# Attention values of two heads as two column tiles of 64 instead of one matmul of 128 columns

## The reference

```python
# first block: 8 sparse heads (values shared by all heads) and 8 forgetting heads
return jnp.einsum('bhqk,bqkd->bqhd', probs, v_sel)      # dsa
return jnp.einsum('bhqs,bshd->bqhd', probs, vb)         # fox
# second block, two layers: 4 heads on a memory of 256 tokens in each, 12 block-sparse heads in layer 1
o = jnp.einsum('bhsm,bmhd->bshd', p, v)                 # mem
return (jnp.einsum('bhcjk,bhcjkd->bhcd', p_sel, v_sel)
        + jnp.einsum('bhck,bhkd->bhcd', p_own, v_own))  # moba
```

## Time and profile before

| | |
|---|---|
| median of 3 runs | 830.77 us (830.05 to 831.02) |
| the profiled execution | 831.16 us |
| its span, first to last instruction | 829.3 us |
| granted clock of PE | 0.997 of full speed |
| PE busy | 817.7 us |
| DVE busy | 522.4 us |
| ACT busy | 427.8 us |

### The profile page before, as it was taken

How to read it: one execution, slowest core, us unless ns; L and a number is a source line. 1 busy time by engine, 2 the same in 40 slices (tenths; PEclk the granted TensorE clock), 3 DMA queues, 4 the chain that set the end, 5 groups by cost and what they waited for, 6 DMA issues and landing times.

```text
span 829.3 us, 11757 instructions
## 1 busy us (share of the span) xinstructions
PE 817.7 (99%) x4514; PEld 700.9 (85%) x4514; DVE 522.4 (63%) x654; ACT 427.8 (52%) x622; POOL 111.3 (13%) x144
## 2 busy tenths in 40 slices
PE   8999999999999999999999999999999999999997
PEld 7998987778878777899999998887667999999996
DVE  5646988767685757556555446687975655555451
ACT  5546656553655554364444444546685654444440
POOL 1600300000021510030000000069900000000000
PEclk9999999999999999999999999999999999999999
DMA  8951444355636633546555555464114466656541
GB/s 298 324 188 40 153 153 152 102 165 203 234 125 234 219 125 102 203 139 217 197 169 191 201 174 183 151 203 136 68 51 153 153 205 214 200 191 196 171 139 52
DMA packets 76503, 140.44 MB, mean 169 GB/s; under 512 B 2952, under 2 KB 22608, under 8 KB 76464
## 3 DMA queue, kind: packets, MB, share of 16 engines
q1 hardware_dynamic: 74352, 134.03, 48.4%
q0 software_dynamic: 1968, 5.82, 2.2%
q10 hardware_dynamic: 144, 0.07, 0.0%
HBM read 138.86 MB, written 1.05 MB: 169 GB/s over the span
## 4 chain that ended last, share of the span: by engine, by line
PE 89%; DVE 6%; ACT 2%; DMA 1%; issue 1%; POOL 0%; SPq 0%; ACTq 0%; DVEq 0%
PE bank L1729 55%; PE bank L2075 22%; PE bank L1877 3%; PE bank L1795 2%; DVE w_lo L1167 2%; PE bank L1931 1%; PE bank L1764 1%; PE bank L1847 1%; DVE tok L1335 1%; PE bank L1907 1%; DMA raw<-in_w_in 1%; PE bank L1932 1%; PE bank L1743 1%; DMA raw<-in_w_mem_kv 1%; DVE mx L1317 1%
## 5 line engine op out<-in xcount | busy, mean ns | idle before, releaser
L1167 DVE TENSOR_TENSOR w_lo<-raw,w_hi 128x2048 fp32r<-128x2048 f32 (+2 forms) x65 | 146.6, 2256 | 50.6 <-ACT w_hi L718 50.1
L1607 DVE TENSOR_TENSOR w_lo<-raw,w_hi 128x2048 fp32r<-128x2048 f32 x48 | 110.0, 2292 | 101.8 <-ACT w_hi L1066 101.8
L718 ACT ACTIVATE w_hi<-raw 128x2048 fp32r<-128x2048 f32 (+2 forms) x64 | 120.6, 1885 | 59.6 <-PE bank L1729 36.1
L1066 ACT ACTIVATE w_hi<-raw 128x2048 fp32r<-128x2048 f32 x48 | 91.9, 1915 | 113.3 <-PE bank L1729 56.3
L1729 PE MATMUL bank<-w_hi,b_hi 128*128 128x512 f32 x376 | 149.0, 396 | 0.1
L1729 PE MATMUL bank<-w_lo,b_hi 128*128 128x512 f32 x376 | 146.6, 390 | 0.0
L1729 PE MATMUL bank<-w_hi,b_lo 128*128 128x512 f32 x376 | 146.5, 390 | 0.0
L1729 PE MATMUL bank<-w_hi,a_hi 128*128 128x512 f32 (+2 forms) x376 | 145.6, 387 | 0.4 <-PE bank L1729 0.4
L2075 PE MATMUL bank<-a_hi,w_hi 128*128 128x256 f32 x512 | 145.1, 283 | 0.0
L2075 PE MATMUL bank<-a_hi,w_lo 128*128 128x256 f32 x512 | 144.9, 283 | 0.0
L2075 PE MATMUL bank<-a_lo,w_hi 128*128 128x256 f32 x512 | 144.9, 283 | 0.0
(11 more groups left out here) (250 smaller groups left out, 915.0 us busy)
## 6 DMA issues: line engine op xcount, KB each, us to landing
raw<-in_w_ff SPq DMA_DIRECT2D x64, 1024.0 KB, 5.1
raw<-in_w_in_moba SPq DMA_DIRECT2D x20, 512.0 KB, 4.3
raw<-in_w_merge SPq DMA_DIRECT2D x8, 1024.0 KB, 5.1
raw<-in_w_out SPq DMA_DIRECT2D x8, 1024.0 KB, 5.1
m<-in_w_in SPq DMA_DIRECT2D x6, 880.0 KB, 8.7
raw<-in_w_in SPq DMA_DIRECT2D x5, 880.0 KB, 8.3
raw<-in_w_mem_kv SPq DMA_DIRECT2D x4, 1024.0 KB, 5.2
raw<-in_w_ple_gate SPq DMA_DIRECT2D x4, 1024.0 KB, 5.0
```

The lines of the kernel that those rows point to most:

```text
L718: act.activation(w_hi[:, slot, 0:n], landing[land][:, 0:n], ACT.Copy).then_inc(hi_ready, 1)
L1066: act.activation(w_hi[:, (base + c) % RING, :], raw[:, (base + c) % RAW, :], ACT.Copy)\
L1167: dve.tensor_tensor(w_lo[:, v % RING, 0:n], landing[land_slot(v)][:, 0:n], w_hi[:, v % RING, 0:n].bitcast(F32), ALU.subtract).then_inc(lo_ ...
L1607: dve.tensor_tensor(w_lo[:, (base + c) % RING, :], raw[:, (base + c) % RAW, :], w_hi[:, (base + c) % RING, :].bitcast(F32), ALU.subtract). ...
```

## The change

The matmul of L1931 is replaced by two, one for each head: the head's 64 columns of values as weights, the head's own 256 probabilities as moving operand, and as output the head's 64 partitions of columns 0 to 255 of the bank. L1932 likewise. An output that starts at partition 0 or 64 with 64 columns of weights places the matmul in the first or second column tile of an array divided into two tiles of 128 rows x 64 columns. The result of a pair now is 128 partitions x 256, and `gate_product`, `out_hi` and `out_lo` are one instruction each instead of two.

```diff
--- before.py
+++ after.py
@@ -890,10 +890,7 @@
                     act.activation(b_hi[:, pair_ktile(pr), :], gated[:], ACT.Copy).then_inc(pair_hi, 1)
                     return
                 act.wait_ge(pv_done, pr + 1)
-                for h in range(2):
-                    rows = slice(HD * h, HD * h + HD)
-                    ins = act.activation(b_hi[rows, pair_ktile(pr), :], b_v[rows, h * S:h * S + S], ACT.Copy)
-                ins.then_inc(pair_hi, 1)
+                act.activation(b_hi[:, pair_ktile(pr), :], b_v[:, 0:S], ACT.Copy).then_inc(pair_hi, 1)
 
             def gate_tanh(g):
 
@@ -1343,11 +1340,7 @@
                 dve.wait_ge(gate_cp, pr + 1)
                 if pr:
                     dve.wait_ge(pair_lo, pr)
-                for h in range(2):
-                    rows = slice(HD * h, HD * h + HD)
-                    ins = dve.scalar_tensor_tensor(gated[rows], b_v[rows, h * S:h * S + S], 0.5, gate_s[rows],
-                                                   ALU.mult, ALU.mult)
-                ins.then_inc(pair_tmp, 1)
+                dve.scalar_tensor_tensor(gated[:], b_v[:, 0:S], 0.5, gate_s[:], ALU.mult, ALU.mult).then_inc(pair_tmp, 1)
 
             def out_lo(n):
 
@@ -1358,11 +1351,7 @@
                     dve.tensor_tensor(b_lo[:, kt, :], gated[:], b_hi[:, kt, :].bitcast(F32), ALU.subtract).then_inc(pair_lo, 1)
                     return
                 dve.wait_ge(pv_done, pr + 1)
-                for h in range(2):
-                    rows = slice(HD * h, HD * h + HD)
-                    ins = dve.tensor_tensor(b_lo[rows, kt, :], b_v[rows, h * S:h * S + S], b_hi[rows, kt, :].bitcast(F32),
-                                            ALU.subtract)
-                ins.then_inc(pair_lo, 1)
+                dve.tensor_tensor(b_lo[:, kt, :], b_v[:, 0:S], b_hi[:, kt, :].bitcast(F32), ALU.subtract).then_inc(pair_lo, 1)
 
             def gate_sum(g):
 
@@ -1925,11 +1914,13 @@
                 if pr:
                     pe.wait_ge(pair_lo, pr)
                 v = pair_cols(pr)["v"]
-                out = b_v[:, :].rearrange("p (h n) -> p h n", h=2)
                 pT = [probT[:, 0:2 * S].rearrange("p (h n) -> p h n", h=2),
                       probT[:, second_keys(n)[1]].rearrange("p (h n) -> p h n", h=2)]
-                pe.matmul(out, v[:, 0], pT[0], start=True, stop=False)
-                pe.matmul(out[:, :, S - w0:S], v[:, 1], pT[1], start=False, stop=True).then_inc(pv_done, 1)
+                for t, c in ((0, 0), (1, S - w0)):
+                    for h in range(2):
+                        rows = slice(HD * h, HD * h + HD)
+                        ins = pe.matmul(b_v[rows, c:S], v[:, t, rows], pT[t][:, h], start=t == 0, stop=t == 1)
+                ins.then_inc(pv_done, 1)
 
             def one_fill(fill_, mid=()):
```

## The result

| | before | after |
|---|---|---|
| median | 830.88 us (4 runs) | 823.41 us (4 runs) |
| lowest to highest | 830.05 to 831.02 | 822.00 to 824.73 |
| ratio of the runs, 95% interval | | 0.9912 (0.9894 to 0.9930) |
| the same pair again, other runs | 830.64 us (17 runs) | 824.41 us (6 runs), 0.9924 (0.9908 to 0.9940) |
| span of the profiled execution | 829.3 us | 820.2 us |

What follows compares the result with a forecast made beforehand. The prediction took PE's stream to bound the kernel nearly everywhere. Overlap -8.6, loads +0.7, switches +5.8 and evacuation -1.2 summed to -3.3 us, from 830.77 to a median of 827.5 us, with a range of 824 to 836.

Steps and rivals of the forecast that it cites:

- What bounds it, and the cost of before: PE's stream is the path nearly everywhere; a group of value matmuls takes 1.29 us, in memory pairs 1.72.
- The overlap: Value matmuls: passes in two column tiles overlap staggered, in program order, gaining 14 x 0.43 + 4 x 0.645 = 8.6 us.
- that case: Staggered overlap in the value groups: head 1's first pass starts with head 0's second; gain 8.6 us, chance 0.45.
- a rival: Full overlap of the tiles in the value groups: -12.5 + 5.8 - 1.2 = -7.9 us, 822.9 us; chance 0.10.
- The loads: Value groups: passes that could start together wait for their own weight loads; 0.7 us taken, between 0 and 1.4.
- The switch: Entering and leaving the divided array around each value group costs 0.32 us, 5.8 us for 18 groups.
- The rule on weight loads: Skill rule: loads overlap a matmul in flight only when row groups differ; a group's eight loads would lie open.
- tiles take turns: Rival for the value groups: no overlap, group stays 1.29 us plus switches, +4.6 us, 835.4 us; chance 0.30.
- The evacuation: One output instruction per pair instead of two removes PE waits, mainly in the last run of heads: 1.2 us saved.
- The bounds: Whole-kernel time between 825.3 and 829.5 us, from loads 0 to 1.4, switch 0.27 to 0.40 a group, evacuation 0.6 to 1.9.
- likeliest case: Staggered overlap in the value groups with a switch like the row tile's: 827.5 us median, chance 0.45.
- The last clause: Last run of heads: the prediction is wrong if PE's saved time becomes waits for DVE, busy 35 of 40 us.

Runs made afterwards that it cites:

- one_tile: Against the changed kernel: both heads' passes in the first column tile, one after another, each evacuation as two instructions; 834.37 us, ratio 1.0053 to before.
- head_order: Against the changed kernel: the same eight passes with head 0's four first, then head 1's; 823.92 us, ratio 0.9919 to before.
- two_evacs: Against the changed kernel: two column tiles kept, but gating, high part and low part each two instructions of 64 partitions again; 828.61 us, ratio 0.9974 to before.
- ahead: Against the changed kernel: a small bf16 matmul of the whole array added in front of each group's first pass; 824.24 us, ratio 0.9920 to before.
- one_tile_merged: Against the changed kernel: both heads' passes in the first column tile, each evacuation one instruction, head 1's result left out; 832.73 us, ratio 1.0027 to before.

## Why the prediction was wrong, step by step

- **What bounds it, and the cost of before.** Right in the main: PE's stream is the path, and two passes of 512 and two of 256 columns take the 1.29 us. The pool mixer is an exception: from its first group of values to its second it takes 8.16 to 8.18 us in all 14 profiles, whether the group is 1.72 us long, longer or shorter, so nothing done to that group shows there.
- **The overlap: the step that failed.** I wrote "If passes start in the order of the program, head 1's first can start only together with head 0's second", and took that case because "the rows show passes starting in program order without exception". All rows of before have passes in one and the same tile, where they follow each other (in one_tile 0.215 us apart); they could not speak on two tiles. The passes of the two tiles start 0.007 us apart, and head_order shows that not even four passes ahead in the program hold them up. The term was 8.6 - 0.7 = 7.9 and is 12.4 us in PE's stream (14 x 0.64 + 4 x 0.86; both are differences of group lengths between one_tile and the changed kernel). These 4.5 us are more than the whole miss: 827.5 was forecast, 823.4 and 824.4 are measured. The case was a rival, with a chance of 0.10, and its time of 822.9 us is nearer to both than the forecast. That it comes so near is in part luck, since its -1.2 for the evacuation is wrong in a way that the points below tell.
- **The loads.** The 0.7 us for loads that can't start early is about 0: the second group of passes starts 0.267 after the first, of which 0.215 are columns and 0.05 the first load, which belongs to the switch.
- **The switch.** Right, in size too: 0.32 us a group was forecast from one row tile, 0.30 is read in the group and 0.31 from one_tile. The rule of the Trainium skill that changing the tiling mode drains TensorE (TensorEngine Tiling (Array Packing), Key Properties) agrees with the trace for column tiles: the load of the first pass starts at 107.96, 0.09 us after the last transpose had streamed its columns, while in before a load starts beside the pass ahead of it.
- **The rule on weight loads** of the Trainium skill (TensorE: Matmul & The Clock Gate, Part 3) did not make the tiles take turns here. All passes have 128 rows, and yet the loads of the third and fourth pass start at 0.054 and 0.060 us, while the first two stream until 0.27; a group of eight with eight loads takes the streaming time of four and the switch. The span model in the same Part 3 of the Trainium skill, by which packed tiles take the time of one, fits: a pair of passes has 0.44 us, one alone 0.43.
- **The evacuation: mis-sized.** I added up the waits that stood in the trace of before and took 1.2 us. That is what merging can be worth beside long groups, as in the trace that it was read from (1.6 to 1.8 in the medians, 0.5 in the stages). Beside short ones it is worth 4.2 (3.5 in the stages). With groups of 0.95 us, PE no longer covers ACT's and DVE's chains in the pool mixer and in the last run of heads: two_evacs takes 6.8 us out of PE's stream and gains 2.0, in the stages 3.1, and PE's waits behind 300 us are 5.2 us instead of 1.9.
- **The sum with the true terms** is -12.4 + 5.6 (18 x 0.31) = -6.8 us for PE's stream. Measured are -6.7 from the first group to PE's last matmul, and -6.2 to -7.5 in the medians. So the merged evacuation adds nothing on top of the stream; it removes the waits of before (1.0) and keeps most of the new ones away. Adding -1.2 for it would have given -8.0, too much. That the sum of waits grows by 0.7 us was not foreseen.
- **The bounds** that the prediction gives for its likeliest case, 825.3 to 829.5, don't follow from its terms: 0 to 1.4, 0.27 to 0.40 for each of 18 groups and 0.6 to 1.9 give -5.6 to -0.6, that is 825.1 to 830.2. The measured times lie outside either way.
- **The last clause** of the forecast, that PE's savings might turn into waits for DVE in the last run of heads, came true in small in the changed kernel (0.6 us for the normalised probabilities, L1896) and at full size in the kernel with two instructions, there for ACT as well.

What stays open: what two tiles of the array divided by rows would do, since the logits have a contraction of 64 for each head. That was not tried.

## What to carry to other kernels

Rows that all have one thing in common (here one tile) don't bear on a rule about two of them; leave such a question open by its bounds, and don't settle it by an order that the rows could not have broken. A shortening of the bounding engine is worth its full price only where the engines beside it have room: ask what they need in the shortened stretch and not only which waits the old trace shows. In a stream like this one, small multiplications by column tiles pay when a group saves more than about 0.3 us, the price of the switch here, so gather as many passes as possible between two changes of tile.

## What the runs showed of the hardware

- Passes in the two column tiles start and stream independently of their order in the program (0.007 us apart in the changed kernel, 0.013 with four passes of the other tile ahead); in one tile they follow each other at 0.215 us for 256 f32 columns.
- Two column tiles stream f32 at full rate beside each other: four pairs of passes in 0.65 us.
- In and out of an array divided by columns costs 0.30 us; in and out of one divided by rows, for one transpose in the kernel before, cost 0.35, loads included. A small bf16 matmul ahead of the change adds only 0.056 us, one between the halves of a group 0.31, of which about 0.26 are one more change out and in.
- One instruction on 128 partitions x 256 takes what one on 64 x 256 takes: 0.417 and 0.422 us on DVE, 0.376 and 0.379 on ACT.
- One transfer differs from execution to execution. The wait of PE around 218 us (for DVE's `b_lo`, behind that transfer) is 0.2 to 1.9 us in the 14 profiles, and the stretch from the eighth group of values to the ninth takes 125.6 to 129.4 us. The chains of the changed kernel and of ahead there:

```profile
206.77 5.26 DMA raw<-in_w_mem_kv
...
218.76 2.74 PE bank L1718 x12
```

```profile
207.58 6.84 DMA raw<-in_w_mem_kv
...
221.16 4.34 PE bank L1718 x12
```

In ahead the transfer took 1.6 us longer, PE waited 1.9 us, and then the same 12 passes took 4.34 us instead of 2.74, at a granted clock of 0.60 in that stretch: part of it ran at the lower level of 1.2 GHz, and it was back at 1.00 in the next. One_tile_merged, whose wait there was 1.9 us too, shows the same: a mean granted clock of 0.94 from 205 to 232 us. That and the start of an execution are why single profiles of these kernels are compared by stages.
